# Hand-overs inside a two-pass MLP: order of the activation sums, place of the waits for low parts

## The reference, cut to what matters

```python
h = _rms_norm(x, norm_mlp[i]) * (1.0 + sc2) + sh2
x = x + g2 * (jnp.square(jax.nn.relu(h @ mlp_w1[i])) @ mlp_w2[i])
```

## Time and profile before

| | |
|---|---|
| median of three runs | 2548.67 us (2546.63 to 2551.38) |
| the profiled execution | 2549.96 us, its span 2548.2 us |
| mean granted TensorE clock | 0.985 |
| TensorE busy | 2445.0 us (96%), 14100 matmuls |
| VectorE busy | 1552.7 us (61%) |
| GpSimd busy | 1031.3 us (40%) |
| ScalarE busy | 793.3 us (31%) |
| DMA, mean | 108 GB/s |

### The profile page before, as it was taken

One profiled execution on the slowest core, in us unless ns is written; L12 is line 12 of the kernel. 1 busy time (PEld: TensorE's weight loads), 2 busy tenths in 40 slices (PEclk: granted clock), 3 DMA queues, 4 the chain that ended last, 5 costly groups with the idle time before them and its releaser, 6 DMA issues.

```text
span 2548.2 us, 38959 instructions
## 1 busy us (share of the span) xinstructions
PE 2445.0 (96%) x14100; PEld 2145.2 (84%) x14100; DVE 1552.7 (61%) x2527; ACT 793.3 (31%) x1244; POOL 1031.3 (40%) x552
## 2 busy tenths in 40 slices
PE   7999999978999999999999999997999998999988
PEld 3978899977888888888888888886888887888877
DVE  6635752264468767777677776577333327777754
ACT  3311122142152222232322322763333334333312
POOL 6125321163113332333323333026565658776730
PEclk9999999989999999999999999998999999999999
DMA  7324533275201221112121121032433355343322
GB/s 255 145 82 142 165 100 109 108 246 200 75 28 56 91 74 58 58 58 99 58 74 58 58 81 51 17 116 78 141 124 123 128 189 199 116 148 116 123 75 83
DMA packets 153348, 274.12 MB, mean 108 GB/s; under 512 B 7428, under 2 KB 105512, under 8 KB 152232
## 3 DMA queue, kind: packets, MB, share of 16 engines
q1 hardware_dynamic: 150288, 263.22, 30.3%
q10 hardware_dynamic: 2968, 9.63, 1.2%
HBM read 204.66 MB, written 63.96 MB: 105 GB/s over the span
## 4 chain that ended last, share of the span: by engine, by line
PE 83%; DVE 8%; issue 3%; POOL 2%; ACT 2%; DMA 2%; ACTq 0%; POOLq 0%; SPq 0%; DVEq 0%
PE bank L455 77%; PE bank L2239 1%; PE bank L2392 1%; DMA ada_st_in<-in_ada_w_dram 1%; PE bank L2304 1%; PE bank L2267 1%; POOL ringL L1369 1%; DVE X L1712 1%; POOL qsF L1586 0%; DVE ada_acc_in L1704 0%; DVE hL L1681 0%; DVE vtok L1758 0%; DVE ada_acc_mlp L1704 0%; DVE xgm L1871 0%; DVE h1L L1878 0%
## 5 line engine op out<-in xcount | busy, mean ns | idle before, releaser
L1712 DVE SCALAR_TENSOR_TENSOR X<-bank,mod,X 128x512 f32<-128x512 f32 (+1 forms) x852 | 545.6, 686 | 270.6 <-PE bank L455 270.2
L1369 POOL TENSOR_TENSOR ringL<-stage,ringH 128x2048 fp32r<-128x2048 f32 x66 | 313.7, 4754 | 661.7 <-ACT ringH L829 633.1
L455 PE MATMUL bank<-hH,ringH 128*128 128x512 f32 (+1 forms) x1248 | 447.2, 358 | 0.2 <-DVE hL L1878 0.2
L455 PE MATMUL bank<-hH,ringL 128*128 128x512 f32 (+1 forms) x1248 | 443.0, 355 | 0.0
L455 PE MATMUL bank<-hL,ringH 128*128 128x512 f32 (+1 forms) x1248 | 442.9, 355 | 0.0
L455 PEld LDWEIGHTS bank<-hH,ringH 128*128 128x128 f32 x1248 | 236.8, 190 | 33.8 <-DVE hL L1878 1.0
L455 PEld LDWEIGHTS bank<-hH,ringL 128*128 128x128 f32 x1248 | 236.5, 190 | 33.2
L455 PEld LDWEIGHTS bank<-hL,ringH 128*128 128x128 f32 x1248 | 236.8, 190 | 32.8
L829 ACT ACTIVATE ringH<-stage 128x2048 fp32r<-128x2048 f32 x65 | 124.0, 1908 | 313.6 <-PE bank L455 311.9
L455 PE MATMUL bank<-ringH,hH 128*128 128x256 f32 x640 | 183.7, 287 | 6.0 <-DVE hL L1681 5.4
L455 PE MATMUL bank<-ringL,hH 128*128 128x256 f32 x640 | 181.6, 284 | 0.0
(11 more groups left out here) (378 smaller groups left out, 5770.3 us busy)
## 6 DMA issues: line engine op xcount, KB each, us to landing
stage<-in_mlp_w_dram SPq DMA_DIRECT2D x64, 1024.0 KB, 5.7
ada_st_mlp<-in_ada_w_dram SPq DMA_DIRECT2D x18, 1536.0 KB, 8.2
stage<-in_ev_w_in_dram SPq DMA_DIRECT2D x14, 1024.0 KB, 5.1
mid_spill<-midT SPq DMA_DIRECT2D x56, 256.0 KB, 2.2
ada_st_in<-in_ada_w_dram SPq DMA_DIRECT2D x8, 1536.0 KB, 9.0
mid_spill<-midB SPq DMA_DIRECT2D x48, 256.0 KB, 2.0
ada<-in_ada_w_dram SPq DMA_DIRECT2D x8, 1024.0 KB, 13.0
x_spill<-X SPq DMA_DIRECT2D x1, 5120.0 KB, 18.5
```

The costliest lines, as they stand in the source:

```text
L455: mm = nc.tensor.matmul(out, a, b, start=first and n == 0, stop=last and n == 2, skip_group_check=chained)
L1369: nc.gpsimd.tensor_tensor(ringL[slot][:, :], stage[:, :], ringH[slot][:, :].bitcast(F32), ALU.subtract).then_inc(w_lo, 1)
L1712: V.scalar_tensor_tensor(out=X[:, d, cols(t)], in0=src[:, 0:TB[t][1]], scalar=gate_ap, in1=X[:, d, cols(t)], op0=ALU.mult, op1=ALU.add).th ...
```

## The change: what it does

1. The full tiles of B11, B12 and B22 get room of their own (12 tiles, in space that the pooling mixer has left), so no tile waits for another. GpSimd makes the four of block 0 as soon as the pooling updates are done and h's low parts are there, then split U_ONE+1, then the eight of block 1, each when its h1L tile is done.
2. VectorE makes G1, G3, G2 whole, one after the other (G2 as G3 + B11), then the hidden sums of chunk 0, then low G1, first half of G4, low G2, low G3, second half of G4, low G4. ScalarE copies G by G, between groups of chunk 1: G1, group 0, G2, group 1, G3, group 2, G4, group 3, the three sum copies, groups 4 and 5.
3. TensorE no longer waits for all of G; each product waits for the four low parts of its own G.
4. GpSimd's sums of chunk 2 wait for its own adds and for two groups of chunk 1, not for G.
5. In the first super-chunk of the second pass VectorE's low parts come one product later.
6. The last super-chunk waits for the first halves of its weights, and for the second halves at its fifth output tile.

```diff
@@ -176,7 +176,9 @@
              "3": ("6", 0), "4": ("4", 1)}
 LOW_AFTER = {"1": [("B22", 0)], "2": [("T4", 0)], "pb": [("B11", 1)], "6": [("B21", 1)], "5": [("p", 1)], "7": [("T2", 1)],
              "3": [("T1", 1)], "4": [("T3", 1)]}
-LOW_FIRST = {**LOW_AFTER, "1": [("T1", 0)], "2": [("T3", 0)], "pa": [("B22", 0)], "pb": [("T4", 0), ("B11", 1)]}
+LOW_FIRST = {**LOW_AFTER, "1": [], "2": [("T1", 0)], "pa": [("T3", 0)], "pb": [("B22", 0), ("T4", 0), ("B11", 1)]}
+G_ORDER = ("G1", "G2", "G3", "G4")
+G_FULL = {"G1": 0, "G2": 2, "G3": 1, "G4": 4}
 S_LOW = ("S2", "S1", "S3", "S4")
 M2_END = PER2 * (NSUP - 1)
 LAST_BANK = (4, 5, 2, 3)
@@ -334,7 +336,7 @@
     out1 = {name: at(f"mid{name}", A_E + 4 + kb, [P, 512]) for name, kb in O_KB.items()}
     u1, u5, out1["B12"], s4 = (at(name, A_AD + 2 * i, [P, 512]) for i, name in enumerate(("u1", "u5", "u2", "s4")))
     u2 = out1["B12"]
-    full_t = (u1, u5, s4)
+    full00, full01, full11 = (at(name, kb, [P, HD, 512]) for name, kb in (("full00", A_M + 8), ("full01", A_M + 16), ("full11", A_M)))
     SUM_KB = ((A_H + 16, A_L + 16), (A_M + 8, A_M + 16))
     qsH = [at(f"qsH{c}", a, [P, 4, 512], F32R) for c, (a, _) in enumerate(SUM_KB)]
     qsL = [at(f"qsL{c}", b, [P, 4, 512], F32R) for c, (_, b) in enumerate(SUM_KB)]
@@ -1211,10 +1213,11 @@
             act.wait_ge(m_act, first_act(ch) + 2 * g + 1)
             nc.scalar.activation(dst, dst, ACT.Square).then_inc(m_act, 1)
 
-        def quarter_hi(k):
-
-            for i, (g, n) in enumerate((("G1", 1), ("G3", 2), ("G2", 3), ("G4", 5))):
-                act.wait_ge(g_full, 5 * k + n)
+        def quarter_hi(i):
+
+            g = G_ORDER[i]
+            for k in range(HD):
+                act.wait_ge(g_full, HD * G_FULL[g] + k + 1)
                 nc.scalar.activation(gH[g][:, k, :], gF[g][:, k, :], ACT.Copy).then_inc(g_hi, 1)
 
         def sum1_hi(ch, i):
@@ -1319,18 +1322,17 @@
             plain_group(0, g)
         split_hi(U_ONE + 2, (m_mm, first_mm(1)), U_ONE % 2)
         quarter_hi(0)
+        plain_group(1, 0)
         quarter_hi(1)
-        plain_group(1, 0)
         plain_group(1, 1)
         quarter_hi(2)
         plain_group(1, 2)
+        quarter_hi(3)
         plain_group(1, 3)
-        quarter_hi(3)
+        for i in (1, 2, 3):
+            sum1_hi(2, i)
         plain_group(1, 4)
         plain_group(1, 5)
-        for i in (1, 2, 3):
-            sum1_hi(2, i)
-        act.wait_ge(g_lo, 4 * HD)
         with act.Fori(1, NSUP - 1) as s:
             first_pass(s, 0)
             first_pass(s, 1)
@@ -1523,13 +1525,11 @@
                                         ALU.subtract).then_inc(p_lo, 1)
 
 
-        def quarter_add(k):
-
-            for j, (tb, d) in enumerate(((0, k), (1, k), (1, HD + k))):
-                if k > 0:
-                    pool.wait_ge(g_full, 5 * (k - 1) + j + 1)
-                nc.gpsimd.tensor_tensor(full_t[j][:, :], h_part(3, 0, d, tb).bitcast(F32), h_part(3, 1, d, tb).bitcast(F32),
-                                        ALU.add).then_inc(g_add, 1)
+        def quarter_add(full, tb, d, k):
+
+            pool.wait_ge(h_lo, GRP * 2 + DT * (1 + tb) + d + 1)
+            nc.gpsimd.tensor_tensor(full[:, k, :], h_part(3, 0, d, tb).bitcast(F32), h_part(3, 1, d, tb).bitcast(F32),
+                                    ALU.add).then_inc(g_add, 1)
 
         def sum1_lo(ch, i):
 
@@ -1612,11 +1612,15 @@
             sum2(s + 1, 4)
 
         pool.wait_ge(w_lo, U_ONE + 1)
+        pool.wait_ge(pool_ev, GRP)
+        for k in range(HD):
+            quarter_add(full00, 0, k, k)
         split_lo(U_ONE + 1, (U_ONE + 1) % 2)
-        pool.wait_ge(h_lo, GRP * 3)
         for k in range(HD):
-            quarter_add(k)
-        pool.wait_ge(g_full, 5 * HD)
+            quarter_add(full01, 1, k, k)
+        for k in range(HD):
+            quarter_add(full11, 1, HD + k, k)
+        pool.wait_ge(g_add, 3 * HD)
         pool.wait_ge(m_mm, first_mm(1) + HT)
         next_sums(2, 0)
         with pool.Fori(1, NSUP - 1) as s:
@@ -2098,25 +2102,35 @@
         norm_tiles(3, 2, 0, DT)
 
 
-        def quarters(k):
-
-            g1, g2, g3, g4 = (gF[g][:, k, :] for g in ("G1", "G2", "G3", "G4"))
-            f00, f01, f11 = (f[:, :] for f in full_t)
-            dve.wait_ge(g_add, 3 * k + 2)
-            V.tensor_tensor(g1, f01, f00, ALU.subtract).then_inc(g_full, 1)
-            dve.wait_ge(g_add, 3 * k + 3)
-            V.tensor_tensor(g3, f11, f01, ALU.subtract).then_inc(g_full, 1)
-            dve.wait_ge(g_full, 5 * k + 1)
-            V.tensor_tensor(g2, f11, g1, ALU.subtract).then_inc(g_full, 1)
-            dve.wait_ge(g_full, 5 * k + 3)
-            V.tensor_tensor(g4, h_part(3, 0, HD + k, 0).bitcast(F32), g2, ALU.subtract).then_inc(g_full, 1)
-            dve.wait_ge(g_full, 5 * k + 4)
-            V.tensor_tensor(g4, g4, h_part(3, 1, HD + k, 0).bitcast(F32), ALU.add).then_inc(g_full, 1)
-
-        def quarter_lo(k):
-
-            for i, g in enumerate(("G1", "G3", "G2", "G4")):
-                dve.wait_ge(g_hi, 4 * k + i + 1)
+        def quarters():
+
+            g1, g2, g3, g4 = (gF[g] for g in ("G1", "G2", "G3", "G4"))
+            dve.wait_ge(x_kept, 32)
+            for k in range(HD):
+                dve.wait_ge(g_add, HD + k + 1)
+                V.tensor_tensor(g1[:, k, :], full01[:, k, :], full00[:, k, :], ALU.subtract).then_inc(g_full, 1)
+            for k in range(HD):
+                dve.wait_ge(g_add, 2 * HD + k + 1)
+                V.tensor_tensor(g3[:, k, :], full11[:, k, :], full01[:, k, :], ALU.subtract).then_inc(g_full, 1)
+            for k in range(HD):
+                dve.wait_ge(g_full, HD + k + 1)
+                V.tensor_tensor(g2[:, k, :], g3[:, k, :], full00[:, k, :], ALU.add).then_inc(g_full, 1)
+
+        def quarter_four(part):
+
+            g2, g4 = gF["G2"], gF["G4"]
+            for k in range(HD):
+                dve.wait_ge(g_full, HD * (2 + part) + k + 1)
+                if part == 0:
+                    V.tensor_tensor(g4[:, k, :], h_part(3, 0, HD + k, 0).bitcast(F32), g2[:, k, :], ALU.subtract).then_inc(g_full, 1)
+                else:
+                    V.tensor_tensor(g4[:, k, :], g4[:, k, :], h_part(3, 1, HD + k, 0).bitcast(F32), ALU.add).then_inc(g_full, 1)
+
+        def quarter_lo(i):
+
+            g = G_ORDER[i]
+            for k in range(HD):
+                dve.wait_ge(g_hi, HD * i + k + 1)
                 V.tensor_tensor(gL[g][:, k, :], gF[g][:, k, :], gH[g][:, k, :].bitcast(F32), ALU.subtract).then_inc(g_lo, 1)
 
         def mid_sums(s, c, d0):
@@ -2196,20 +2210,17 @@
                     else:
                         mid_low(s + ahead, name)
 
-        for k in range(2):
-            if k == 0:
-                dve.wait_ge(x_kept, 32)
-            quarters(k)
+        quarters()
+        dve.wait_ge(m_act, first_act(1))
+        mid_sums(0, 0, first_dve(0))
         quarter_lo(0)
-        for ch in range(PLAIN):
-            dve.wait_ge(m_act, first_act(ch + 1) if ch + 1 < PLAIN else 12 * PLAIN)
-            mid_sums(0, ch, first_dve(ch))
-            if ch == 0:
-                quarters(2)
-                quarter_lo(1)
-                quarters(3)
-                quarter_lo(2)
-                quarter_lo(3)
+        quarter_four(0)
+        quarter_lo(1)
+        quarter_lo(2)
+        quarter_four(1)
+        quarter_lo(3)
+        dve.wait_ge(m_act, 12 * PLAIN)
+        mid_sums(0, 1, first_dve(1))
         with dve.Fori(1, NSUP - 1) as s:
             first_pass(s, 0)
             first_pass(s, 1)
@@ -2685,6 +2696,8 @@
             a0, d0, slot = first_act(ch), first_dve(ch), (U_ONE + c) % 2
 
             def quarter_product(out, w_name, part, first):
+                if part[0] == "G":
+                    pe.wait_ge(g_lo, HD * (G_ORDER.index(part) + 1))
                 for k in range(HD):
                     wH, wL = first_weight(slot, w_name, k)
                     if part[0] == "G":
@@ -2762,12 +2775,14 @@
 
             s = NSUP - 1
             names = {0: ("B11", "B21"), 1: ("T1", "B22"), 2: ("p", "p")}
-            pe.wait_ge(w_lo, W_PASS + 4 * s + 4)
+            pe.wait_ge(w_lo, W_PASS + 4 * s + 2)
             for i, (t, d) in enumerate(BY_END):
                 if d == 0:
                     pe.wait_ge(f_lo, F_PASS + 8 * s + {2: 3, 0: 3, 1: 5}[t])
                 pe.wait_ge(m2_ev[1], max(M2_END + i - 3, M2_END - 4 + i % 4 + 1) if i >= 4 else M2_END - 4 + (i % 4 + 1 if i > 1 else 0))
                 for c in range(2):
+                    if i == HD:
+                        pe.wait_ge(w_lo, W_PASS + 4 * s + c + 3)
                     for k in range(HT):
                         wH, wL = second_weight(c, f"A{1 + d // HD}{k + 1}", d % HD)
                         if t == 2:
@@ -2781,7 +2796,6 @@
 
         plain_chunk(0)
         plain_chunk(1)
-        pe.wait_ge(g_lo, 4 * HD)
         with pe.Fori(1, NSUP - 1) as s:
             first_pass(s, 0)
             first_pass(s, 1)
```

## The result

The changed kernel takes 2528.73 us (median of 4 runs, 2525.03 to 2534.82); the kernel before, run beside it, 2548.99 (4 runs, 2546.63 to 2551.38). The ratio is 0.9926, 95% interval [0.9913, 0.994]: 20.3 us faster. The forecast was 2527.5, and faster.

A forecast was written before the change was run, and what follows sets the result against it. The prediction took TensorE, busy 96% of the span, as the bound. Gains of 10.0, 3.3 and 7.9 us at three hand-overs sum to 21.2, taking the median of 2548.67 to 2527.5 us; range 2521 to 2535.5.

The forecast's parts named there:

- stop of G4L and its clock removed: Before A11: the 15.3 us wait for G4's last low part and 2.2 us of lower clock go, 17.5 us.
- h1L beside adds: Ahead of chunk 1: GpSimd's early adds delay six of VectorE's h1L by 0.4 us each, costing 2.4 us.
- new wait before A11: Late G4 copies on ScalarE hold up group 5's relu, so TensorE waits 3.1 us; bounds 0 and 7.
- clock behind it: Behind the new wait before A11 TensorE runs at the lower clock, costing 2.0 us; bounds 0 and 2.2.
- first hand-over: Before the first super-chunk: 17.5 us at stake less 2.4, 3.1 and 2.0, a gain of 10.0 us.
- second hand-over: Second pass, first round: eviction wait replaced by 4.1 us before pb; gain 3.3 us, bounds 2.5 and 4.7.
- third hand-over: Last super-chunk: products start on first-half weights, 0.4 us wait left; gain 7.9 us, bounds 6.5 and 8.1.
- part 2: First hand-over: early GpSimd adds delay VectorE's h1L ahead of chunk 1, costing 2.4 us; bounds 0 and 3.5.
- rival on the slower side: Chunk 0's fifth group: slow feeding takes TensorE to 1.2 GHz, and it stays there; slower, 2554 at 150 matmuls; chance 0.02.
- first rival: First hand-over: splits and low parts fall apart luckily, the first wait goes altogether; 5.1 us more, 2522.4; chance 0.17.
- second rival: First hand-over, the ScalarE road is long: VectorE meets all adds and splits, wait 7 to 9 us, 2532 to 2535; 0.20.
- The rule of the Trainium skill: VectorE instructions with two SBUF inputs and GpSimd's SBUF readers exclude each other whole; makes the early adds cost 2.4 us.

The follow-up runs named there:

- second hand-over undone: Changed kernel with the old places of the low parts in the second pass's first round; 2530.07 us, ratio 0.992.
- third undone: Changed kernel with the old wait, for all four halves of the weights, before the last super-chunk; 2536.83 us, ratio 0.9945.
- second halves early: Changed kernel with the second halves of the first w2 block made right behind the first halves, ahead of the sums; 2532.57 us, ratio 0.995.
- adds behind the norm: Changed kernel with GpSimd's eight adds of block 1 waiting for the whole norm of that block; 2531.66 us, ratio 0.9935.
- adds behind the norm with the G4 copies last: Changed kernel with block 1's adds after the whole norm and ScalarE's G4 high copies behind group 5; 2524.6 us, ratio 0.9906.
- T1 later: Changed kernel with the first w2 block's second halves made ahead of the sums and T1's low part moved behind pa's evictions; 2524.51 us, ratio 0.9904.
- the next version: Changed kernel with w2 second halves ahead of the sums, T1's low part behind pa's evictions, and ScalarE's G4 copies last; 2527.1 us, ratio 0.9906.
- the version that keeps the gain: Changed kernel with w2 second halves ahead of the sums and T1's and T3's high copies ahead of ScalarE's sum copies; 2523.78 us, ratio 0.9905.

## Why the prediction was right, step by step

| term | predicted | measured | from |
|---|---|---|---|
| stop of G4L and its clock removed | 17.5 | 17.4 | 15.31, and 7.68 (A11 to S1 G1) against 5.62 at 2.4 GHz |
| h1L beside adds | -2.4 | -2.4 | chunk 1 at 21.62 (second hand-over undone) against 19.26 |
| clock ahead of chunk 1 | not priced | -1.6 | 23.22 against 21.62 |
| new wait before A11 | -3.1 | -2.1 | 1744.14 |
| clock behind it | -2.0 | -1.5 | 7.15 against 5.62 |
| **first hand-over** | **10.0** | **9.8** | 69.92 - 60.10 |
| **second hand-over** | **3.3** | **3.0** | 32.48 - 29.45 |
| **third hand-over** | **7.9** | **7.8** | 345.07 - 337.24 |
| sum | 21.2 | 20.7 | |

- *h1L beside the adds.* As the prediction's part 2 has it: 0.40 us on each of five rows in the middle, 0.3 on the first and the last two together, and 0.75 again when the adds wait. What it left out is that TensorE, fed one k step per 1.9 us there, fell to 1.2 GHz behind these waits, for eight matmuls of chunk 0 (steps of 0.43 us from 1706.7 to 1709.7). It did so in three traces of the nine that have the early adds in the changed kernel's place (chunk 1 at 23.2), not in the other six (21.6). The prediction gave this clock only to its rival on the slower side, where it was to last; it cost 1.6 us and was over.
- *The wait before A11* came by the road named, ScalarE's order, G4 copies first, and went when the copies were moved. 2.06 us in place of 3.1, because chunk 1 itself had started 1.6 later: where it had not, the wait was 3.3 (second or third undone, second halves early). The two trade against each other (1.6 against 1.2), so the sum hardly shows either.
- *G3L beside the split.* Four low parts took 10.02 us; alone they take 2.5. One took 5.10 us beside the split and two 1.77 beside the adds behind it, just as the prediction counted them. It had G4 whole at 1743.8, which is 47.6 from the norm's last sum; it was at 48.5. Its 8.4 us for the twelve G sums were 9.5, which cost nothing, since VectorE then stood idle for 1.48 us before the first G3L.
- *The clock behind a short stop.* No row of before had a stop so short, and the prediction took the full price of the long ones: 2.0. It was 1.5, behind 2.06 us, and 1.5 again behind 3.3 us (59.73 - 52.56 = 7.17 against 5.62). That a stop as short as 2.06 cost any clock was not sure beforehand: others of its length cost none (last section).
- *The second hand-over.* The eviction wait is gone and one of 3.72 us (4.1 predicted) stands before pb, for the second-half split as said. Of the 3.8 us between 7.49 and 3.72, some 1.0 went to a wait that the prediction doesn't have, 1.29 us in place of 0.3 inside product 1. It was 0.33 in one of the later runs and 1.03 in another with the same order there; its cause wasn't looked for.
- *The third.* 0.51 us of wait (0.4 predicted), no lower clock behind it.
- *The total.* The chain gives 20.7 us, and 20.3 stand between the medians. That the first term came out at 9.8 is better than its parts deserve: the clock ahead of chunk 1 (1.6) was not priced, and a wait 1.0 and a clock 0.5 smaller than priced made up for it. The shorter wait follows from the later start, the smaller clock is luck.
- *The range.* With part 2 at its lower bound of 0, the first rival would be at 2520.1 and not at 2521; and its second rival's own numbers (17.5 - 3.5 - 7 to 9 - 2.0) leave a gain of 3 to 5 us at the first place, not 4 to 6. Neither bears on the outcome.

The rivals: the first wait did not go altogether, the ScalarE road was not long (though with the adds behind the norm it was, 10.1 us), and the clock came back each time within a few microseconds.

The rule of the Trainium skill that the prediction weighed (SBUF — State Buffer, Who interferes with whom; for an instruction with a single SBUF input the section excepts the two-port performance modes, which the prediction leaves out) agrees with the runs: 1.15 against 0.75 for the h1L with and without an add in its way, while four evictions, which read PSUM, took 2.71 us beside GpSimd's low parts and its next split (changed kernel, at 2130.67), 0.68 us each as before.

## What to carry to other kernels

A stop at a hand-over goes only if the engine behind it is not itself queued behind something new; three times here (adds behind the norm with the G4 copies last, second halves early, T1 later) the time saved at one wait came back, in part or more than whole, as a wait at another hand-over of the same stretch. So read the queue of each engine for what stands in front of the instruction that releases TensorE, and move that, as with the G4 copies and T1's high part: a high copy that waits for its data should not stand ahead of copies whose data are there. And VectorE's operations on two SBUF tiles should not be placed beside a train of GpSimd operations when an eviction is queued behind them.

## What the runs showed of the hardware

- **VectorE can lose to GpSimd for nine instructions in a row.** T1's low part of 14.08 us is of a kind that takes 1.21 us alone (T3's, at 2128.40). GpSimd went through eight low parts at 10.09 / 8 = 1.26 us each, as if alone, and through two splits; the first of the ten was over when VectorE's instruction began at 2112.83, the second was running, and eight more started while it stood. It happened again, with 14.13 us, in the next version. In the version that keeps the gain the same eight took 14.01 us and VectorE's own 2.0 to 2.3 each: there they took turns. What decides between the two was not tried. The page named above says that the loser blocks for the whole instruction of the other, which both agree with.
- **A stop of TensorE of some 2 us may cost the clock or not.** No row of the profile before shows one so short. Before A11 the clock fell to the lower level behind 2.04, 2.06 and 2.07 us (three traces), and before pa behind 2.17 us in one trace; but behind 2.15 us before pa in two others it stayed at 2.4 GHz, and so it did behind 1.95 and 1.96 before S2 G2 and behind 1.68 to 1.72 before pa. TensorE's timeline behind the one in the version that keeps the gain (the row of 2107.73 above) has the step of 0.12 us that 256 columns take at 2.4 GHz:

```profile
2108.16 0.28 PE L457 MATMUL bank<-inpH,ringH 128*128 128x256 f32 x1
2108.28 0.28 PE L457 MATMUL bank<-inpL,ringH 128*128 128x256 f32 x1
```

From the norm on, all stops of 3.27 us and longer cost clock, and none of 1.45 us and shorter did, but for this: behind waits of under 1 us that came three times in a row, at 1702 to 1706, it fell in three traces of nine with the same order of work, with 1.6 us between the two. So such a stop is to be priced with a chance, not as free and not as certain.
